# Routing tail of three expert layers: first pass's rows by a 0/1 product, slots inside its gate product, modulation rows loaded at two times

## The chip, the core and the metric

One program on one core of a Trainium2 chip. The time is the device time of the whole program in microseconds (us); lower is better. The profiler records one execution: every instruction of the engines PE (matrix products), DVE (vector), ACT (scalar), POOL (general) and SP (issues loads and stores), and every DMA packet.

## The reference, cut to what matters

A block with a mixer and a mixture of experts, then two more layers (attention and a mixture of experts each) whose inputs are scaled and shifted by rows made from a condition vector `c`. There are 512 tokens of 1024 numbers, 16 experts, and each token goes to two experts of one group.

```python
mod = c_act @ w_ada[i] + b_ada[i]
sh1, sc1, g1, sh2, sc2, g2 = [m[:, None, :] for m in jnp.split(mod, 6, axis=-1)]
...
group_p, group_idx = lax.top_k(jax.nn.softmax(group_logits, axis=-1), 1)
exp_p, exp_idx = lax.top_k(jax.nn.softmax(in_group, axis=-1), TOP_K_IN_GROUP)
combine = jnp.sum(jax.nn.one_hot(expert_id, N_EXPERTS) * gate[..., None], axis=1)
h = jax.nn.silu(jnp.einsum("td,edf->tef", t, expert_w_gate)) * jnp.einsum("td,edf->tef", t, expert_w_up)
y = jnp.einsum("tef,efd->td", h * combine[:, :, None], expert_w_down)
```

## The kernel before, in words

All is float32; one product of 128x128 by 512 columns is two PE instructions. The program is a row of blocks in which each engine has its own list of instructions, written out in order; engines wait for one another by semaphores. Within an engine nothing overtakes.

An expert layer is the function `moe` (L1303), called three times: in the first block (with `mod=0`), in the fox layer (`mod=1`) and in the last layer (no `mod`). The text calls them the first, second and third expert layer. It has two blocks.

The first block makes the normalised rows `x_tok`, stores them to `x_rows` in memory (SP, L1656), and routes: DVE finds each token's two experts (chain "route"), PE counts with triangular and all-one matrices which place a token has in its expert's list (the **ranks**, L1466 and L1468, in `bank[7]`). Then the tail of the routing: DVE turns ranks to 0/1 rows over 128 places (chain "pick", L1591), PE multiplies them with token numbers (L1475), and DVE has the token of each place of experts 0 and 1 (`slot_tok`, L1600). POOL gathers pass 0's and pass 1's rows by it from `x_rows` (`load_x`, L2081). Chains "order", "slots" and "expert" sort the other twelve experts by their counts and give each token a place in a **pass**.

A pass is 128 rows: one expert of up to 128 tokens or two of up to 64. There are 13, numbered 0 to 12 (`PASSES`). Passes 2 to 12 get their rows from four gathers of quarter rows each (L2076), whose addresses (`part_rows`) come from two small PE products, `pass_slots` (L1829) and `parts` (L1836). In the second block PE runs, for each pass `e`: the gate and up product (`gate_up`, L1708, eight steps of k), the down product of the pass before (`end`, L1721), the turn of this pass's hidden rows (`turn_h`, L1713). Ahead of pass 0 it makes `pass_slots`, the turn of pass 0's gathered rows (`turn_x`, L1693) and `parts`, with filler products (`keep_clock`, L1864) between them. DVE's list in that block is `slots_of_passes`, `rows_of_tokens`, `weights_of_tokens` (L2002 to L1994 in the order of the run), then for each pass the product of gate and up (`times_up`, L1732), the next pass's rows, the copies of the outputs (L1740, L1741) and of the turned rows (L1735). ACT applies silu (L1729) and issues the expert weights on its own DMA queue, each when its place of five is free: the gate and up weights after the gate product of the place's last user, the down weights after its down product. Outputs of a pass are stored by ACT (L1909) from one of two buffers, so the copies of pass 10 wait for pass 8's store to land.

In the first two layers SP also loads what the next layer's modulation needs (`modulation_loads`, L1291): 1536 of `b_ada` to each of four partitions, and six blocks of 128x1024 partial sums (`ada_part`), which it issues when the gate product of pass 10 is done and the last expert's gate and up weights have landed; in the first layer two norm rows (`ln2_loads`) follow, then the next stage's first weights. DVE adds the bias (`add_bias`, L2046, two steps each behind passes 11 and 12), waiting for all these loads:

```python
BIAS_AT = {NP - 2: (0, 1), NP - 1: (2, 3)}
...
slots_of_passes()
rows_of_tokens()
weights_of_tokens()
for e in range(NP):
    body(e)
```

## Time and profile before

| what | value |
|---|---|
| runs (3) | 2012.82, 2014.77, 2016.58 us; median 2014.77 |
| the profiled execution | 2019.38 us; its span 2017.6 us |
| PE busy | 1926.7 us, 95% of the span |
| DVE, ACT, POOL busy | 951.1, 435.5, 326.8 us |
| mean granted clock of PE | 0.979 of full |
| moved by DMA | 363.87 MB, 180 GB/s in the mean |

The span runs from the first to the last instruction; the execution's own time has 1.8 us more around it. A busy PE is one that has a product in flight, at whatever clock; the granted clock is given apart. The mean of the DMA hides that it is idle in the attention stages and full in the expert layers.

### The profile page before, as it was taken

What the parts mean: (1) busy time and instruction counts of PE and PEld (TensorE: products, weight loads), DVE (VectorE), ACT (ScalarE), POOL (GpSimd) and SP (SyncE); (2) the same over time, 40 slices, a digit from 0 to 9 for tenths busy, and PEclk for the clock granted to TensorE, in tenths of its full rate; (3) what the DMA queues carried; (4) which work ended last, traced back from release to release, by engine and by line L of the source; (5) the groups of instructions that cost most, each with busy time, mean ns of one, the idle gap of its engine ahead of it and who ended that gap; (6) DMA issues with size and microseconds to landing.
All of it is one profiled execution on the core that took longest, in us unless ns stands there. A gap on an engine that the chain in (4) does not pass through costs nothing. (4 is left out here: it accounts for less than half of the span.)

```text
span 2017.6 us, 20813 instructions
## 1 busy us (share of the span) xinstructions
PE 1926.7 (95%) x7482; PEld 1022.3 (51%) x7482; DVE 951.1 (47%) x1803; ACT 435.5 (22%) x1051; POOL 326.8 (16%) x548
## 2 busy tenths in 40 slices
PE   8999999999999999999799998999997999999995
PEld 4444444558885444543345445545433656645441
DVE  3443734547776022633363555535334367625333
ACT  1111101013333100110151105511001546612000
POOL 1000000000002000133010006502332003301333
PEclk9999999999999999999898999999997999999997
DMA  5222373730003125599844782137996202046996
GB/s 193 102 104 103 137 257 114 255 137 1 1 1 124 45 103 196 198 345 391 335 154 146 273 331 85 56 153 274 351 412 259 70 24 84 2 169 247 331 406 248
DMA packets 123401, 363.87 MB, mean 180 GB/s; under 512 B 26572, under 2 KB 31976, under 8 KB 110752
## 3 DMA queue, kind: packets, MB, share of 16 engines
q1 hardware_dynamic: 83200, 196.16, 27.0%
q10 hardware_dynamic: 26064, 133.70, 16.9%
q0 software_dynamic: 14032, 32.64, 4.6%
q8 instruction: 62, 1.02, 0.2%
q14 instruction: 43, 0.35, 0.1%
HBM read 335.07 MB, written 39.88 MB: 186 GB/s over the span
## 5 line engine op out<-in xcount | busy, mean ns | idle before, releaser
L447 PE MATMUL bank<-featT,ring 128*128 128x512 f32 x384 | 170.4, 597 | 3.0 <-DMA ring<-in_w_in 3.0
L2583 PE MATMUL bank<-ring,featT 128*128 128x512 f32 x384 | 168.9, 601 | 2.2 <-DVE small L2675 1.6
L1416 PE MATMUL bank<-ring,work 128*128 128x512 f32 x384 | 166.5, 593 | 3.0 <-PEq L1198 1.0
L1708 PE MATMUL bank<-work 128*128 128x512 f32 x384 | 168.8, 592 | 0.0
L2076 POOL DMA_INDIRECT work<-x_rows,small x132 | 131.7, 998 | 218.4 <-DVE work L2040 155.4
L2583 PEld LDWEIGHTS bank<-ring,featT 128*128 128x128 f32 x384 | 73.5, 193 | 93.4 <-issue 91.6
L1416 PEld LDWEIGHTS bank<-ring,work 128*128 128x128 f32 x384 | 72.2, 190 | 91.2 <-issue 91.2
L1732 DVE TENSOR_TENSOR work<-work,bank 128x256 f32<-128x256 f32 x39 | 16.5, 422 | 213.9 <-ACT work L1729 213.8
L447 PEld LDWEIGHTS bank<-featT,ring 128*128 128x128 f32 x384 | 71.8, 192 | 85.0 <-issue 81.9
L1708 PEld LDWEIGHTS bank<-work 128*128 128x128 f32 x384 | 71.1, 190 | 80.4 <-issue 80.4
L546 PE MATMUL bank<-ring,featT 128*128 128x512 f32 x256 | 110.4, 593 | 0.9 <-PEq L427 0.9
L1708 PE MATMUL bank<-ring,work 128*64 128x512 f32 (+1 forms) x384 | 106.2, 595 | 0.8 <-DVE work L1726 0.8
L1721 PE MATMUL bank<-work 128*128 128x512 f32 x184 | 88.6, 624 | 1.8 <-DVE work L1735 1.8
L1729 ACT ACTIVATE work<-bank 128x256 f32<-128x256 f32 x39 | 14.9, 383 | 323.4 <-PE bank L1708 323.4
L1100 PE MATMUL bank<-ring,featT 128*128 128x512 f32 x192 | 83.3, 593 | 1.0 <-PEq L830 1.0
L546 PEld LDWEIGHTS bank<-ring,featT 128*128 128x128 f32 x256 | 48.5, 190 | 61.4 <-issue 61.4
L301 DVE SCALAR_TENSOR_TENSOR ring_halves<-ring_halves,ismall 128x1024 f32<-128x1024 f32 x48 | 61.6, 1283 | 34.2 <-DMA ring_halves<-in_w_ada 30.7
L468 DVE TENSOR_SCALAR work<-bank,small 128x512 f32<-128x512 f32 x24 | 18.0, 751 | 107.6 <-PE bank L447 107.6
L1708 PEld LDWEIGHTS bank<-ring,work 128*64 128x64 f32 (+1 forms) x384 | 37.9, 150 | 60.5 <-issue 60.5
L2040 DVE STREAM_TRANSPOSE work<-work 128x1024 f32<-128x1024 f32 x33 | 66.9, 2028 | 0.0
L1721 PEld LDWEIGHTS bank<-work 128*128 128x128 f32 x184 | 35.6, 199 | 51.0 <-issue 51.0
L1100 PEld LDWEIGHTS bank<-ring,featT 128*128 128x128 f32 x192 | 36.1, 190 | 44.7 <-issue 44.7
(507 smaller groups left out, 3067.2 us busy)
## 6 DMA issues: line engine op xcount, KB each, us to landing
ring<-in_w_in SPq DMA_DIRECT2D x15, 2048.0 KB, 11.6
ring_halves<-in_w_ada SPq DMA_DIRECT2D x48, 512.0 KB, 6.5
y_rows<-work ACTq DMA_DIRECT2D x39, 512.0 KB, 11.6
state<-in_w_ada SPq DMA_DIRECT2D x24, 512.0 KB, 6.8
ada_w<-in_w_ada SPq DMA_DIRECT2D x24, 512.0 KB, 6.5
ring<-in_fox_w_in SPq DMA_DIRECT2D x6, 2048.0 KB, 11.7
work<-in_moe_w_gate ACTq DMA_DIRECT2D x12, 1024.0 KB, 7.2
work<-in_moe_w_up ACTq DMA_DIRECT2D x12, 1024.0 KB, 10.4
```

The lines of the kernel that those rows point to most:

```text
L301: DV.done(nc.vector.scalar_tensor_tensor(out=acc, in0=w, scalar=c_cols[:, k:k + 1], in1=acc, op0=ALU.mult, op1=ALU.add), ("slab", i))
L447: last = nc.tensor.matmul(bank[b % 4][:, :], w[:, k, (b % 4) * P:(b % 4 + 1) * P], featT[:, k, :], start=(k == 0), stop=(k == KD - 1))
L468: DV.done(nc.vector.tensor_scalar(acc, src[:, :], conv_cols[:, CONV - 1, b:b + 1], None, ALU.mult), ("tap0", b))
L546: last = nc.tensor.matmul(uv_bank(j)[:, :], featT[:, k, t * P:(t + 1) * P], w[:, k, :], start=(k == 0), stop=(k == KD - 1))
L1100: last = nc.tensor.matmul(zg_bank(j)[:, :], featT[:, k, t * P:(t + 1) * P], w[:, k, :], start=(k == 0), stop=(k == KD - 1))
L1416: last = nc.tensor.matmul(bank[j % 4][:, :], outT[:, k, t * P:(t + 1) * P], w[:, k, :], start=(k == 0), stop=(k == KD - 1))
L1708: last = nc.tensor.matmul(gu_sum[par][at], xgT[par][:, k, at], w_gu[place_of[u]][:, k, :, :], start=(k == 0), stop=(k == KD - 1))
L1721: last = nc.tensor.matmul(y_bank(e, h)[at, :], hT[par][:, k, at], w_dn[place_of[u]][k][:, span(h)], start=(k == 0), stop=(k == KF - 1))
L1732: return nc.vector.tensor_tensor(h_tok[par], act_g[par], bank[2 + par][:, FF:2 * FF], ALU.mult)
L2040: nc.vector.transpose(xgT[par].rearrange("p k (s b) -> p s k b", s=NQ), xg[par].rearrange("p (s a k) -> p s k a", s=NQ, k=KD)).then_inc(M_ ...
L2076: nc.gpsimd.indirect_dma_start(out=xg[par][:, s * QD:(s + 1) * QD], out_offset=None, in_=x_quarters, in_offset=bass.IndirectOffsetOnAxis(a ...
L2583: last = nc.tensor.matmul(f_bank(j)[:, :], featT[:, k, t * P:(t + 1) * P], w[:, k, :], start=(k == 0), stop=(k == KD - 1))
```

## The change

For each of the three expert layers:

- `x_rows` places of experts 0 and 1 are kept as one 0/1 matrix each, `is_listed` (places along the columns, tokens along the rows). Pass 0's rows are no longer gathered: PE multiplies the normalised rows by `is_listed[0]` (`first_rows`), 8 blocks by 4 token tiles, which gives them turned already. `slot_tok` holds pass 1's tokens alone (`second_list`).
- The chains "slots" and "expert" move to the second block, and the copy of pass 0's rows and `slot_tok` stand among them. `pass_slots` and `parts` move inside pass 0's gate product, ahead of its steps k = 4 and k = 6. Of the nine filler products behind the ranks, seven go.
- The partial sums 4 and 5 (after the norm rows in the first layer) are issued after the down product of pass 4; 0 to 3 when the gate product of pass 10 is done, with no wait for the last expert's weights. The bias steps are 1024 wide: one behind pass 9, one behind pass 10, three behind pass 11, one behind pass 12.

```diff
-        def modulation_loads(sp, l, places_free):
-            for i in range(4):
-                load(sp, b_ada[32 * i:32 * i + 1, :], D["b_ada_2"][l:l + 1, i * B_ADA:(i + 1) * B_ADA])
+        def modulation_loads(sp, l, after_fifth, places_free):
+            for i in range(6):
+                sp.dma_start(b_row(i), D["b_ada_2"][l:l + 1, i * DM:(i + 1) * DM]).then_inc(first_rows_landed, 16)
...
+            after_fifth()
+            for i in (4, 5):
+                sp.dma_start(ada_sum[:, i * DM:(i + 1) * DM], ada_part[l, :, i * DM:(i + 1) * DM]).then_inc(first_rows_landed, 16)
             places_free()
-            for i in range(6):
+            for i in range(4):
                 load(sp, ada_sum[:, i * DM:(i + 1) * DM], ada_part[l, :, i * DM:(i + 1) * DM])
...
-            BIAS_AT = {NP - 2: (0, 1), NP - 1: (2, 3)}
+            BIAS_AT = {NP - 4: (4,), NP - 3: (5,), NP - 2: (0, 1, 2), NP - 1: (3,)}
...
-                    keep_clock(2)
-                    for a in range(2 * T):
...
-                    keep_clock(4)
+                    keep_clock(1)
...
-                    link(V.tensor_tensor(two(prod2), two(O12), bcast(ranks.unsqueeze(1), P, 2, T * NE), ALU.mult))
-                    link(V.reduce_sum(rank_of, prod2.rearrange("p (a n) -> p a n", n=NE), X_AXIS))
...
+                    link(V.scalar_tensor_tensor(out=slot_at, in0=t16(ranks)[:, :, 0:N_WHOLE], scalar=1.0, in1=t16(O5[:, 0:T * NE])[:, :, 0:N_WHOLE], op0=ALU.add, op1=ALU.mult))
+                    for i in range(N_WHOLE):
+                        link(V.scalar_tensor_tensor(out=is_listed[i].rearrange("p (t n) -> p t n", t=T), in0=bcast(iota.unsqueeze(1), P, T, P), scalar=1.0,
+                                                    in1=bcast(slot_at[:, :, i:i + 1], P, T, P), op0=ALU.add, op1=ALU.is_equal))
...
+                    link(G.memset(xg[0], 0.0))
...
-                def gate_up(e, par):
+                def gate_up(e, par, between={}):
                     for k in range(KD):
+                        if k in between:
+                            between[k]()
...
+                    def first_rows():
+                        DV.wait(pe, ("pick", 1))
+                        for k in range(KD):
+                            for t in tiles:
+                                last = nc.tensor.matmul(bank[k // 4][:, (k % 4) * P:(k % 4 + 1) * P], eighth(x_tok[:, t, :], k), is_listed[0][:, t * P:(t + 1) * P],
+                                                        start=(t == 0), stop=(t == T - 1))
+                        last.then_inc(M_xT.sem, 1)
+
+                    def second_list():
+                        DV.wait(pe, ("pick", 2))
+                        for t in tiles:
+                            last = nc.tensor.matmul(bank[6][:, P:P + 1], is_listed[1][:, t * P:(t + 1) * P], tok_id[:, t:t + 1], start=(t == 0), stop=(t == T - 1))
+                        PE.done(last, "slots")
...
-                        gate_up(e, par)
+                        gate_up(e, par, {4: pass_slots, 6: parts} if e == 0 else {})
...
-                    keep_clock(1)
-                    pass_slots()
-                    keep_clock(1)
-                    turn_x(pe, 0, 0, 0)
-                    parts()
+                    first_rows()
+                    second_list()
                     keep_clock(1)
...
-                        def places_free():
-                            sp.wait_ge(M_gu.sem, v(M_gu, pass_of[users[3][-1]]))
-                            wait_gate_up(sp, NE - 1)
-                        modulation_loads(sp, mod, places_free)
-                    if late:
-                        late(sp)
+                        def after_fifth():
+                            sp.wait_ge(M_down.sem, v(M_down, pass_of[users[4][-1]]))
+                            if late:
+                                late(sp)
+                        modulation_loads(sp, mod, after_fifth, lambda: sp.wait_ge(M_gu.sem, v(M_gu, pass_of[users[3][-1]])))
...
+                    act.wait_ge(x_stored, 16 * T * (nth + 1))
                     keep_x_act(0)
...
+                    def slots_and_experts():
...
+                        dve.wait_ge(x_stored, 16 * T * (nth + 1))
+                        keep_x_dve(0)
+                        PE.wait(dve, "slots")
+                        DV.done(V.tensor_copy(slot_tok, bank[6][:, P:P + 1]), "slot_tok")
...
                         DV.done(V.tensor_copy(slot_f, bank[6][:, 2 * P:2 * P + NP]), "slot_f")
-                        keep_x_dve(0)
                         PE.wait(dve, "parts")
...
+                    slots_and_experts()
                     slots_of_passes()
                     rows_of_tokens()
                     weights_of_tokens()
...
-                    load_x(0, 0)
                     load_x(1, 1)
```

How the instructions move, at three places. On PE, first expert layer, from the start of the second block; L1864 is the filler product, L1829 `pass_slots`, L1693 the turn of gathered rows, L1836 `parts`, L1708 the gate product. Before:

```order
L1864 MATMUL bank<-level_mask,ident 128x512
L1829 MATMUL bank<-featT,work 128x13 [waits dve_steps]
L1829 MATMUL bank<-featT,work 128x13 x3
L1829 MATMUL bank<-featT,work 128x13 [waits dve_steps]
L1829 MATMUL bank<-featT,work 128x13 x3
L1864 MATMUL bank<-level_mask,ident 128x512
L1693 MATMUL bank<-ident,work 128x128 [waits moe_x_landed0]
L1693 MATMUL bank<-ident,work 128x128 x7
L1836 MATMUL bank<-featT 128x13 [waits act_steps,dve_steps]
L1836 MATMUL bank<-featT 128x13 x3
L1864 MATMUL bank<-level_mask,ident 128x512
L1708 MATMUL bank<-ring,work 128x512 [waits moe_x_kept_act,moe_x_kept_dve,slot0_landed]
```

Now, from the second step of the gate product (L1680) on; L1801 is `pass_slots`, L1808 `parts`, L1663 the turn of pass 1's rows, L1685 the turn of pass 0's hidden rows:

```order
L1680 MATMUL bank<-ring,work 128x512 x3
L1801 MATMUL bank<-featT,work 128x13 [waits dve_steps]
L1801 MATMUL bank<-featT,work 128x13 x3
L1801 MATMUL bank<-featT,work 128x13 [waits dve_steps]
L1801 MATMUL bank<-featT,work 128x13 x3
L1680 MATMUL bank<-ring,work 128x512 x2
L1808 MATMUL bank<-featT 128x13 [waits act_steps,dve_steps]
L1808 MATMUL bank<-featT 128x13 x3
L1680 MATMUL bank<-ring,work 128x512 x2
L1663 MATMUL bank<-ident,work 128x128 [waits moe_x_landed1]
L1663 MATMUL bank<-ident,work 128x128 x7
L1685 MATMUL bank<-ident,work 128x128 [waits moe_h]
```

Slots and parts have gone from ahead of the gate product to between its steps.

On DVE, first expert layer, the second block from its first chain's last step to the part rows; L1698 is the copy of pass 0's rows, L1971 `slot_tok`, L1975 the slots' 0/1 rows, L2013 the copy of the slots, L2015 and L2017 the part rows:

```order
L1967 SCALAR_TENSOR_TENSOR featT<-featT 128x8 [waits dve_steps]
L1698 COPY work<-bank 128x512 [waits moe_x_turned,moe_x_stored,dve_steps]
L1971 CAST ismall<-bank 128x1 [waits pe_steps]
L1972 TENSOR_TENSOR featT<-featT,small 128x104
L1973 TENSOR_TENSOR featT<-featT,small 128x104 [waits dve_steps]
L1975 TENSOR_TENSOR work<-work,featT 128x512 [waits dve_steps] x2
L1977 TENSOR_TENSOR featT<-featT,small 128x144 [waits dve_steps]
L1978 TENSOR_REDUCE featT<-featT 128x12 [waits dve_steps]
L1979 CAST ismall<-featT 128x12 [waits dve_steps]
L2013 COPY featT<-bank 128x13 [waits pe_steps,dve_steps]
L2015 TENSOR_SCALAR featT<-bank,small 128x52 [waits pe_steps]
L2017 CAST small<-featT 128x52 [waits dve_steps]
```

Before, the slots and experts stood at the end of the first block (L1622 is their last step), and the second began with the copy of the slots (L1999), pass 0's rows (L1726) and the part rows (L2002):

```order
L1621 TENSOR_REDUCE featT<-featT 128x12 [waits dve_steps]
L1622 CAST ismall<-featT 128x12 [waits dve_steps]
L1965 UNCONDITIONAL_BRANCH [waits dve_steps]
L1999 COPY featT<-bank 128x13 [waits pe_steps]
L1726 COPY work<-bank 128x512 [waits moe_x_turned]
L2002 TENSOR_SCALAR featT<-bank,small 128x52 [waits pe_steps]
L2004 CAST small<-featT 128x52 [waits dve_steps]
```

Slots and experts have come in ahead of the copy of the slots. What follows the part rows on DVE is the same in both: rows and weights of tokens, then `times_up` of pass 0.

On SP, first expert layer, from the norm row on (L202 is the helper `load`, L1302 the two early sums). Before:

```order
L202 DMA featT<-in_ffn_norm 128x1024
L202 DMA work<-ada_part 128x1024 [waits moe_gate_up_sum,far_gate_up_landed0,ada_stored1,ada_stored0]
L202 DMA work<-ada_part 128x1024 x5
L202 DMA work<-in_ln_g 128x1024
L202 DMA work<-in_ln_b 128x1024
L120 DMA ring<-in_fox_w_in 128x8x512 [waits moe_gate_up_sum]
```

Now:

```order
L202 DMA featT<-in_ffn_norm 128x1024
L202 DMA work<-in_ln_g 128x1024 [waits moe_down_sum,ada_stored1,ada_stored0]
L202 DMA work<-in_ln_b 128x1024
L1302 DMA work<-ada_part 128x1024 x2
L202 DMA work<-ada_part 128x1024 [waits moe_gate_up_sum]
L202 DMA work<-ada_part 128x1024 x3
L120 DMA ring<-in_fox_w_in 128x8x512 [waits moe_gate_up_sum]
```

Two norm rows and two sums have moved ahead, to the wait for a down product; the wait for landed weights is gone.

## Rows read from the trace of the kernel before

**Rows 1.** Windows; after each engine's busy us: PEclk, DMA share, GB/s.
```profile
912.00:977.00 65.00, 65.00 (x206) 25.89 (x205) 20.93 (x25) 5.88 (x12) 19.95 (x20) 1.00 1.01 406
1533.00:1540.30 7.30, 6.62 (x10) 2.60 (x10) 5.12 (x5) 0.00 (x0) 0.00 (x0) 0.60 0.18 72
```

**Rows 2.** Timeline, first expert layer's routing and pass 0: start, us, engine, line.
```profile
837.23 0.45 PE L1466 MATMUL bank<-work,strict 128*128 128x80 f32 x2 [0.32 <-DVE work L1579]
...
839.27 1.42 DVE L1591 TENSOR_TENSOR work<-work,small 128x512 f32<-128x512 f32 x2
...
851.16 0.27 DVE L2002 TENSOR_SCALAR featT<-bank,small 128x52 f32<-128x52 f32 x1
...
851.92 7.03 PE L1708 MATMUL bank<-ring,work 128*128 128x512 f32 x16
...
858.88 0.17 DVE L1994 CAST ismall<-small 128x8 int32<-128x8 f32 x1
...
859.95 0.44 PE L1713 MATMUL bank<-ident,work 128*128 128x128 f32 x2
```

**Rows 3.** Timeline of PE, 128x128 products back to back.
```profile
537.00 1.95 PE L868 MATMUL bank<-work 128*128 128x128 f32 x16
```

**Rows 4.** Timeline of PE, second expert layer: ranks, then pass 0's turn.
```profile
1373.81 0.45 PE L1466 MATMUL bank<-work,strict 128*128 128x80 f32 x2 [0.32 <-DVE work L1579]
...
1398.70 0.44 PE L1713 MATMUL bank<-ident,work 128*128 128x128 f32 x2
```

**Rows 5.** Timeline of PE, third expert layer: the same two places.
```profile
1837.33 0.45 PE L1466 MATMUL bank<-work,strict 128*128 128x80 f32 x2 [0.33 <-DVE work L1579]
...
1860.01 0.44 PE L1713 MATMUL bank<-ident,work 128*128 128x128 f32 x2
```

**Rows 6.** Timeline, first expert layer, passes 10 to 12.
```profile
963.79 0.38 ACT L1729 ACTIVATE work<-bank 128x256 f32<-128x256 f32 x1 [6.63 <-PE bank L1708]
...
970.53 3.19 SPq L202 DMA_DIRECT2D work<-ada_part  x6
...
978.11 7.03 PE L1708 MATMUL bank<-work 128*128 128x512 f32 x16
...
979.08 0.69 DVE L1741 COPY work<-bank 128x512 f32<-128x512 f32 x1 [1.84 <-DMA y_rows<-work]
...
993.63 3.52 DVE L2046 TENSOR_TENSOR work<-work,featT 1x1536 f32<-1x1536 f32 x2 [13.53 <-DMA work<-in_ln_b]
...
997.67 0.69 PE L1713 MATMUL bank<-ident,work 128*128 128x128 f32 x2 [8.95 <-DVE work L1732]
```

**Rows 7.** Timeline of PE, first expert layer, last down products, whole.
```profile
998.97 5.67 PE L1721 MATMUL bank<-work 128*128 128x512 f32 x8 [0.61 <-DVE work L1735]
```

**Rows 8.** Timeline, second expert layer, the same passes.
```profile
1508.53 2.82 SPq L202 DMA_DIRECT2D work<-ada_part  x6
...
1516.85 7.03 PE L1708 MATMUL bank<-work 128*128 128x512 f32 x16
1517.16 1.29 DVE L1740 TENSOR_TENSOR work<-bank,work 128x512 f32<-128x512 f32 x2 [1.18 <-DMA y_rows<-work]
...
1533.05 0.69 PE L1713 MATMUL bank<-ident,work 128*128 128x128 f32 x2 [5.58 <-DVE work L1732]
...
1534.34 5.93 PE L1721 MATMUL bank<-work 128*128 128x512 f32 x8 [0.61 <-DVE work L1735]
```

**Rows 9.** Timeline of PE, third expert layer, pass 12 (no modulation there).
```profile
1978.17 7.03 PE L1708 MATMUL bank<-work 128*128 128x512 f32 x16
...
1989.76 3.67 PE L1721 MATMUL bank<-work 128*128 128x512 f32 x8 [0.61 <-DVE work L1735]
```

**Rows 10.** DMA queues, 970.6 to 974: q1 is SP's, q10 ACT's, q0 POOL's.
```profile
q10 hardware_dynamic: 367, 1.39, 101.3%
```

**Rows 11.** DMA queues, 974 to 983: packets, MB, share of 16 engines.
```profile
q1 hardware_dynamic: 556, 2.06, 55.9%
q10 hardware_dynamic: 477, 1.72, 46.8%
```

More of the change, by code:

```diff
@@ L1470, in _ @@
                     PE.done(last, "ranks")
-                    keep_clock(2)
-                    for a in range(2 * T):
-                        if a in (0, T):
-                            DV.wait(pe, ("pick", N_PICK - 2 + a // T))
-                        last = nc.tensor.matmul(bank[6][:, P:P + N_WHOLE], slot_is[:, a * P:(a + 1) * P], tok_of[:, a * N_WHOLE:(a + 1) * N_WHOLE], start=(a == 0), stop=(a == 2 * T - 1))
-                    PE.done(last, "slots")
-                    keep_clock(4)
+                    keep_clock(1)
                 @block.scalar
```

86 lines of the change are left out of this document (44 added, 42 removed).

## The prediction

> **What bounds the kernel now.** I read the page's busy times first, then the windows, then the timeline of the three expert layers, PE and DVE side by side. PE is busy in 95% of the span, and inside the passes it is the bound: in the stretch 912 to 977 it is busy in every microsecond at the full clock, while the 16 DMA engines are full too, 406 GB/s at a share of 1.01 [rows 1]. So time can be won or lost in two sorts of places only: where PE waits, or where a load comes later than its use. The change touches two. One is the routing ahead of pass 0: from the ranks (L1466, 837.23) to the turned gate product of pass 0 (L1713, 859.95) 22.7 us go by in the first expert layer [rows 2], 22.7 in the third [rows 5], 24.9 in the second [rows 4]. The other is the end of the first two layers: there PE stands idle for 8.95 us [rows 6] and 5.58 us [rows 8] ahead of the last turn, because DVE has the bias rows in front of the last pass's product and the rows have not landed (the row at 993.63 waited 13.53 us for a load). The third layer, which has no modulation, shows the same passes without it [rows 9].
>
> **Routing, to the start of pass 0.** Removed are five DVE steps and a gather with its eight turns; added are one small step and two 512-wide comparisons. Two such comparisons took 1.42 us, from 839.27 on [rows 2] and behind two small steps; with one step ahead of them the first list is ready at about 839.5. Then PE makes pass 0's rows: 32 products of 128x128, two instructions each. Sixteen such instructions took 1.95 us of which about 0.28 is the last one's length, so 0.111 us each [rows 3]; 64 take 7.1 us, and the rows stand in the bank at 846.9. Copying them (0.7) hides beside the second list (8 x 0.111 = 0.9) and one filler product (about 0.95); the gate product starts at about 848.6 in place of 851.92 [rows 2]: 3.3 us earlier.
>
> **Routing, inside pass 0.** The 24 instructions for slots and parts, which stood ahead of the gate product, now stand inside it: 24 x 0.111 = 2.7 us. So it ends at 848.6 + 7.0 + 2.7 = 858.3, about 0.6 us earlier than before. The parts end at 856.6, after three quarters of the product (5.2) and the 2.7. What matters is who waits for them. On DVE everything from the part rows to the last cast of the weights of tokens stands, before and after, between the parts and the product of gate and up that PE's turn needs (the order on DVE). That stretch lasts from 851.16 to 859.05, 7.9 us [rows 2]; before, it lay beside the whole gate product and ended with it. Now it starts 5.5 us later, because the parts come at the sixth of eight steps. It ends at 864.5, the product of gate and up 0.5 later, and PE turns at 865.05 in place of 859.95: **+5.1 us**. ACT has no say: its two exponentials and its table load lie inside the same stretch. Every later pass moves with it, since PE is full there. The third layer has the same pace, +5.1. In the second the stretch took 2.2 us longer before; I take the new one at the pace of the others, since 64 wide products replace the light ones there: +2.9. Sum **+13.1**.
>
> **The clock after that wait.** PE has its gate product and the turn of pass 1 done at 859.2 and then nothing for 5.8 us. No stretch before has such a gap in the middle of a layer; the nearest is the 5.58 us at the second layer's end [rows 8]. After it the mean granted clock was 0.60 of full speed, so mostly the lower level, 1.2 GHz [rows 1], and the turn took 0.69 and the eight down instructions 5.93, against 0.44 [rows 2] and 3.67 [rows 9]: 2.5 us. Bounds: 0 if the clock holds; 3.5 if a whole gate product (7.03) runs at half. I take 2.5, the row with the nearest gap: three times, **+7.5** (0 to 10.5).
>
> **The modulation rows.** Before, six rows (and in the first layer two norm rows) were issued when the last expert's weights had landed, 970.53 and 1508.53 [rows 6, 8]. From the last gate product's start to the last down product's end the first layer needs 998.97 + 5.67 - 978.11 = 26.5 us [rows 6, 7], the second 23.4 [rows 8], the third 15.3 [rows 9]. All that could be won is 11.2 and 8.1. But the bytes stay the same. Four loads of 0.52 MB (first layer; two in the second) now go out after the fifth pass, where the engines are full; at 406 GB/s they take 5.2 us (2.6), by which all later loads of ACT's queue come later. The other four go out when pass 10's gate product ends, 963.8, and no longer wait for the last expert's weights. SP's traffic appeared 3.5 us after its issue [rows 6, 10], and then the two queues shared the engines about evenly, 55.9% and 46.8% [rows 11].
> First layer: at 967.3 the last expert's weights had 3.2 us to go; with the 5.2 that makes 8.4, at half speed beside 5.2 of SP's, then beside the next stage's weights. They land between 980.9 (if those keep out) and 984, and PE wants them at 978.1 [rows 6]: about 5 late. The output of pass 8, whose landing (979.08) frees the buffer for pass 10's, lands at 979.1 - 2.5 (what SP had taken before) + 3 x 5.2 = 992.2, so the down products of pass 11 start at about 992.9 in place of 985.1: 7.8 late in all. The five idle microseconds lower the clock, 2. New: 15.3 + 7.8 + 2 = 25.1, **-1.4**.
> Second layer: the weights land as they are wanted, pass 8's output at 1517.2 - 2.6 + 2.6 + 5.2 + 2.9 = 1525.3, with its copy 2.8 late; 1 for the clock. New 19.1, **-4.3**. Bounds for both: nothing won, or all 19.3.
> The Trainium skill (DMA: Bandwidth & Descriptors, Where 436 GB/s comes from) holds that between HBM and SBUF the HBM's share of about 358 GB/s binds. The trace shows more, 406 GB/s over 65 us [rows 1], and the measurement decides; with 358 each 5.2 would be 5.9, an estimate, and the sum some 3 us higher.
>
> **At no cost, with their cover.** The memset of the row buffer and the missing gather lie on POOL, idle at that time. Pass 1's gather starts later but has the longer pass 0 ahead of its turn; were that gone, its flight would show. The quarter gathers of passes 2 on start 5 us later, for a use a pass later; the fifth expert's weights 1 us later, for a use four passes later. The wait for the stored rows ended long before the copies. The four early bias steps lie where DVE idles in each pass.
>
> **Sum.** 13.1 + 7.5 - 1.4 - 4.3 = +14.9. The profiled execution took 2019.38, its span 2017.6; it would take 2034. The median of the three runs lies 4.6 below it, so I forecast 2014.77 + 14.9 = **2029.7 us**. A measurement of this kernel can tell about 0.2%, 4 us, from no change.
>
> **The rivals.**
> *The rows are hidden in full.* The weights of experts 13 to 15 and pass 8's output land in time in spite of the earlier loads; it decides at 978.1 and 985.1 in the first layer. For it: no PE wait on a load inside a layer, and 7.6 us between landing and use for the last weights [rows 6]. Against it: the full engines [rows 1, 11]. Then the ends give 19.3: 13.1 + 7.5 - 19.3 = +1.3, 2016, no change; if the clock holds as well, -6.2, 2008.6, faster.
> *The clock holds through the routing wait.* Place: the 5.8 us behind pass 0's gate product. Against it stands the 5.58 us gap. +7.4, 2022.
> *Loads late in more passes.* The 5.2 us of backlog also delays experts 9 to 14, each wait with its clock; price the upper bounds, 13.1 + 10.5 and nothing won, about +24, 2039.
> *The slots hide as named.* The move inside the gate product would cost only its 2.7 us if DVE's tail came behind pass 0's product of gate and up. The order excludes it, so it has no chance of its own.
>
> **How the numbers follow.** My forecast 0.54 (its own range 2022 to 2037), the rows hidden 0.27, of which 0.14 faster, 0.12 the same and 0.01 slower, the clock holding 0.10, more loads late 0.09. Faster 0.14, same 0.12, slower 0.74. The range 2008.5 to 2041 takes in all four cases and leaves out a tenth or so at the two ends.
>
> **What would show it.** Right: in each layer a PE wait of 5 to 6 us ahead of pass 0's turn, ended by DVE, and slow products behind it; no bias step that waits for a load; in the first layer a wait for weights at pass 12. Wrong: pass 0's turn at most 23 us after the ranks (then the DVE stretch is not what PE waits for), or the last pass as short as in the third layer, 15.3 (then the loads do not collide).

## The result, and the profile after

The changed kernel takes 2049.07 us (median of 4 runs, 2048.18 to 2053.36), the kernel before 2014.67 (4 runs): **1.75% slower**, ratio 1.0175 with an interval of 1.0157 to 1.0192. The forecast was 2029.7 with a range up to 2041. The side was right, the size was not: +34.4 us where +14.9 stood. One execution of those behind all the numbers here, of the run s_fill6 below, took 4102.86 us, twice the others, for a reason not known, and stands in no median and no ratio. The profiled execution took 2049.17 us with a span of 2047.4; against the profiled execution of before, whose own time lay 4.6 above its median, the span grew by 29.8. Cut at places that both kernels have, it grew here (us):

| stretch | before | after | difference |
|---|---|---|---|
| start to the ranks of the first layer | 837.2 | 836.1 | -1.1 |
| ranks to the turn of pass 0, first layer | 22.72 | 35.85 | +13.1 |
| that turn to the last gate product | 118.2 | 122.8 | +4.6 |
| last gate product to the end of the last down product | 26.5 | 22.1 | -4.5 |
| on to the ranks of the second layer | 369.2 | 365.5 | -3.6 |
| ranks to turn, second layer | 24.89 | 35.85 | +11.0 |
| turn to last gate product | 118.2 | 120.8 | +2.6 |
| last gate product to the end | 23.4 | 17.3 | -6.1 |
| on to the ranks of the third layer | 297.1 | 296.1 | -1.0 |
| ranks to turn, third layer | 22.68 | 35.83 | +13.2 |
| turn to the end of the span | 157.6 | 159.2 | +1.6 |

The -3.6 lies in the fox layer, which the change does not touch: from its first projection to the next ranks the profiles of these kernels take between 344.5 and 348.5, and the one of before, 348.2, is near the upper end. The rest is the routing, three times, and the ends of two layers.

First the routing, PE's timeline in the first layer, which answers to [rows 2] (start, us, engine, line, tiles and shapes, count; in brackets the idle time ahead and what ended it):

```profile
836.13 0.45 PE L1471 MATMUL bank<-work,strict 128*128 128x80 f32 x2 [0.32 <-DVE work L1577]
...
838.48 15.50 PE L1815 MATMUL bank<-work,resid 128*128 128x128 f32 x64
...
855.57 3.60 PE L1680 MATMUL bank<-ring,work 128*128 128x512 f32 x8
...
865.12 1.04 PE L1663 MATMUL bank<-ident,work 128*128 128x128 f32 x8
871.98 0.69 PE L1685 MATMUL bank<-ident,work 128*128 128x128 f32 x2 [5.82 <-DVE work L1704]
872.63 9.86 PE L1680 MATMUL bank<-ring,work 128*128 128x512 f32 x16
```

L1815 is `first_rows`: its 64 instructions take 15.50 us where the forecast had 7.1, and the gate product starts 19.4 us behind the ranks, 8.1 later than the forecast had it (848.6 less 837.23, 11.4). Behind that, all is as forecast: a wait of 5.82 ahead of the turn, ended by DVE, and a slow gate product of pass 1. The second and third layer show the same 15.50 and 5.8. A product has two operands: the stationary block, whose load is an instruction of its own (PEld), and the moving operand, whose columns the product's instruction counts. The loads, by shape, from 800 to 1000 us (busy us, mean ns):

```profile
L1680 PEld LDWEIGHTS bank<-work 128*128 128x128 f32 x125 | 23.1, 190 | 28.1 <-issue 26.1 <-DMA work<-in_expert_w_up 2.0
L1815 PEld LDWEIGHTS bank<-work,resid 128*128 128x128 f32 x64 | 15.3, 335 | 0.9 <-DVE work L1584 0.9
```

A block of the same shape is loaded in 190 ns by the gate products and in 335 ns here, one behind the other without a pause. DVE's timeline of the same stretch:

```profile
843.56 0.17 DVE L1967 SCALAR_TENSOR_TENSOR featT<-featT 128x8 f32<-128x8 f32 x1
854.12 0.69 DVE L1698 COPY work<-bank 128x512 f32<-128x512 f32 x1 [10.39 <-PE bank L1815]
...
863.51 0.27 DVE L2015 TENSOR_SCALAR featT<-bank,small 128x52 f32<-128x52 f32 x1 [2.37 <-PE bank L1808]
...
871.30 0.17 DVE L2008 CAST ismall<-small 128x8 int32<-128x8 f32 x1
871.50 0.42 DVE L1704 TENSOR_TENSOR work<-work,bank 128x256 f32<-128x256 f32 x1
```

DVE waits 10.39 us for these rows, with the last slots steps behind the copy; from the part rows (863.51) to the last cast of the weights (871.47) it takes 8.0 us, against the 7.9 of [rows 2]. Windows of the rows, of the wait and of what follows it. The last three numbers are the granted clock, the DMA share and the rate in GB/s:

```profile
838.40:846.00 7.60, 7.52 (x32) 7.52 (x32) 4.53 (x18) 0.00 (x0) 0.00 (x0) 1.00 0.01 2
846.00:854.00 8.00, 8.00 (x37) 8.00 (x36) 0.00 (x0) 0.00 (x0) 0.00 (x0) 1.00 0.00 0
866.00:872.00 6.00, 0.18 (x3) 0.02 (x1) 5.21 (x25) 2.58 (x5) 4.63 (x5) 0.95 0.77 277
872.00:878.00 6.00, 6.00 (x9) 2.57 (x10) 0.95 (x2) 0.00 (x0) 2.41 (x3) 0.50 0.86 312
```

The clock was full, 1.00, while the rows were made, so their double time is no fall of the clock, and the DMA was idle beside them. Behind the wait the clock is at the lower level, 1.2 GHz, for six microseconds. Pass 1's gate product takes 9.86, 9.81 and 8.61 in the three layers, and 7.03 at the full clock.

Last the ends of the first two layers, PE's timeline, against [rows 6 to 8]:

```profile
994.78 7.13 PE L1680 MATMUL bank<-work 128*128 128x512 f32 x16 [1.79 <-DMA work<-in_expert_w_up]
1005.85 6.34 PE L1693 MATMUL bank<-ring_halves,work 128*64 128x512 f32 x16 [3.94 <-DVE work L1707]
...
1013.17 3.67 PE L1693 MATMUL bank<-work 128*128 128x512 f32 x8 [0.61 <-DVE work L1707]
...
1539.01 7.03 PE L1680 MATMUL bank<-work 128*128 128x512 f32 x16
1547.70 3.65 PE L1693 MATMUL bank<-ring_halves,work 128*64 128x512 f32 x16 [1.66 <-DVE work L1707]
...
1552.65 3.67 PE L1693 MATMUL bank<-work 128*128 128x512 f32 x8 [0.61 <-DVE work L1707]
```

The 8.95 and 5.58 us ahead of the last turn are gone. New are a wait of 1.79 for the last expert's weights and waits of 3.94 and 1.66 ahead of the down products of pass 11; behind the longer one these products take 6.34 in place of 3.65.

### The profile page after: what moved, and what is told of

The parts are those of the page before. It is cut to its first block and busy times, and to the rows that moved or that the text cites. A ratio compares the mean times of both kernels' runs of the same rounds, so it can differ in the third digit from the quotient of the medians.

```text
span 2047.4 us, 21023 instructions
## 1 busy us (share of the span) xinstructions
PE 1948.2 (95%) x7584; PEld 1052.2 (51%) x7584; DVE 949.4 (46%) x1801; ACT 435.5 (21%) x1051; POOL 330.5 (16%) x548
## 5 line engine op out<-in xcount | busy, mean ns | idle before, releaser
L1680 PE MATMUL bank<-work 128*128 128x512 f32 x384 | 168.9, 593 | 1.8 <-DMA work<-in_expert_w_up 1.8
L1680 PE MATMUL bank<-ring,work 128*64 128x512 f32 (+1 forms) x384 | 114.6, 616 | 0.0
L1680 PEld LDWEIGHTS bank<-work 128*128 128x128 f32 x384 | 71.1, 190 | 82.4 <-issue 80.4
L1693 PE MATMUL bank<-work 128*128 128x512 f32 x184 | 84.4, 598 | 1.8 <-DVE work L1707 1.8
L1680 PEld LDWEIGHTS bank<-ring,work 128*64 128x64 f32 (+1 forms) x384 | 40.2, 158 | 61.3 <-issue 61.3
L1693 PE MATMUL bank<-ring_halves,work 128*64 128x512 f32 (+1 forms) x192 | 57.1, 627 | 5.6 <-DVE work L1707 5.6
## 6 DMA issues: line engine op xcount, KB each, us to landing
ring<-in_fox_w_in SPq DMA_DIRECT2D x6, 2048.0 KB, 11.4
work<-in_moe_w_up ACTq DMA_DIRECT2D x12, 1024.0 KB, 10.9
```

The source lines that it names most:

```text
L1680: last = nc.tensor.matmul(gu_sum[par][at], xgT[par][:, k, at], w_gu[place_of[u]][:, k, :, :], start=(k == 0), stop=(k == KD - 1))
L1693: last = nc.tensor.matmul(y_bank(e, h)[at, :], hT[par][:, k, at], w_dn[place_of[u]][k][:, span(h)], start=(k == 0), stop=(k == KF - 1))
```

## The experiments

Times are medians; a ratio is to runs of the kernel before on the same chip, whose median was 2016.6 to 2017.7 in these groups. The groups ran on different chips, so two runs of different groups are compared by their ratios; 0.001 of a ratio is 2 us.

### Why the rows took 15.5 us

One run (e_probe) measures the product by itself. Behind the ranks of the kernel before, runs of 32 products each, `every(x, k, s)` being 128 numbers of a row in steps of s:

```diff
+ for k in range(KD):
+     for t in tiles:
+         nc.tensor.matmul(bank[0][:, (k % 4) * P:(k % 4 + 1) * P], every(x_tok[:, t, :], k, 8), ident[:, :], start=(t == 0), stop=(t == T - 1))
```

and so with the other steps, with `start=True, stop=True` for single products, and once with the two operands exchanged.

> The kernel before, with seven extra runs of 32 products of 128x128 (64 instructions each) behind the ranks; their sums are thrown away, nothing else is changed. Stationary blocks: first layer, every 8th number of the normalised rows, once adding four products to a sum and once each product alone; second layer, neighbouring numbers, every 2nd number, and a run with the 0/1 unit matrix as stationary block and every 8th number as the moving operand; third layer, every 4th number adding up, and neighbouring numbers each alone. Theory S (the step of the stationary block sets the time): 15.5 us for both runs with step 8, 7.1 for neighbouring numbers and for the moving operand, steps 2 and 4 in between or at 7.1. Rival A (adding four products to one sum sets it): 15.5 for every run that adds up, whatever the step, 7.1 for the two runs of single products. Rival F (a new stationary block for every product sets it): 15.5 for all but the run with the unit matrix.

Measured, PE's timeline (L1483 step 8 adding up, L1486 step 8 each alone, L1490 neighbouring numbers, L1493 step 2, L1496 moving operand with step 8, L1500 step 4, L1503 neighbouring numbers each alone):

```profile
838.92 15.47 PE L1483 MATMUL bank<-ident,resid 128*128 128x128 f32 x64
854.24 15.40 PE L1486 MATMUL bank<-ident,resid 128*128 128x128 f32 x64
...
1406.20 7.39 PE L1490 MATMUL bank<-ident,work 128*128 128x128 f32 x64
1413.43 7.70 PE L1493 MATMUL bank<-ident,work 128*128 128x128 f32 x64
1420.97 15.09 PE L1496 MATMUL bank<-work,ident 128*128 128x128 f32 x64
...
1900.02 15.18 PE L1500 MATMUL bank<-ident,work 128*128 128x128 f32 x64
1915.03 7.31 PE L1503 MATMUL bank<-ident,work 128*128 128x128 f32 x64
```

The step decides; adding up and new blocks do not (rivals A and F fall: step 8 takes as long without adding up, and a new block for every product costs nothing with neighbouring numbers). Neighbouring numbers and step 2 take 7.3 to 7.7, steps 4 and 8 twice that. Theory S was wrong in two points. Step 4 pays in full, where 15.5 stood for step 8 alone. And the moving operand pays as much, 15.09; there the loads of the unit matrix stay at 209 ns, so it is not the load of the stationary block as such but the reading of either operand.

In the changed kernel itself, the same instructions on neighbouring numbers (run contig):

```diff
-  gu = [(lambda s, i=i: s[:, :].rearrange("p (g k n) -> p g k n", g=2, k=KD)[:, i, :, :], rows8(w[u]))
+  gu = [(lambda s, i=i: s[:, :].rearrange("p (g k n) -> p g k n", g=2, k=KD)[:, i, :, :], rows(w[u]) if u == 0 else rows8(w[u]))
...
-  last = nc.tensor.matmul(bank[k // 4][:, (k % 4) * P:(k % 4 + 1) * P], eighth(x_tok[:, t, :], k), is_listed[0][:, t * P:(t + 1) * P],
+  last = nc.tensor.matmul(bank[k // 4][:, (k % 4) * P:(k % 4 + 1) * P], x_tok[:, t, k * P:(k + 1) * P], is_listed[0][:, t * P:(t + 1) * P],
```

> The changed kernel with the stationary blocks of pass 0's rows made of 128 neighbouring numbers in place of every 8th, and expert 0's gate and up weights loaded in the row order that fits this; as many instructions of the same shapes. Theory: the step of 8 is all that made these 64 instructions take 15.5 us. They take 7.4, pass 0's turn comes 28 us behind the ranks in place of 35.8, and the kernel takes 2049 - 3 x 8 = about 2025, a little under the forecast. Rival: the loads of expert 0 in 1 KB rows come late or the products are slow for another reason, and it stays above 2040.

Measured: 2025.62 us, ratio 1.0044 (1.0029 to 1.0058). PE's timeline, first layer, whose ranks stood at 834.78:

```profile
837.12 7.41 PE L1815 MATMUL bank<-work,resid 128*128 128x128 f32 x64
...
862.53 0.69 PE L1685 MATMUL bank<-ident,work 128*128 128x128 f32 x2 [5.80 <-DVE work L1704]
863.17 9.39 PE L1680 MATMUL bank<-ring,work 128*128 128x512 f32 x16
```

27.75 us from ranks to turn, where the forecast had 27.8 (837.23 to 865.05). With this one price put right, the turn, the wait and the slow product come out as forecast. The whole time does not quite: +8.9 against this group's runs of before (2016.73), where the forecast had +14.9; the modulation part gave more than the forecast allowed it (below).

The other way round, with the rows as moving operand, 512 neighbouring numbers at a time (run swap):

```diff
-  for k in range(KD):
-      for t in tiles:
-          last = nc.tensor.matmul(bank[k // 4][:, (k % 4) * P:(k % 4 + 1) * P], eighth(x_tok[:, t, :], k), is_listed[0][:, t * P:(t + 1) * P],
-                                  start=(t == 0), stop=(t == T - 1))
+  for h in range(2):
+      for t in tiles:
+          last = nc.tensor.matmul(bank[h][:, :], is_listed[0][:, t * P:(t + 1) * P], x_tok[:, t, span(h)], start=(t == 0), stop=(t == T - 1))
```

ACT and DVE copy a half each to `xg[0]`, and eight turns follow, as for gathered rows.

> The changed kernel with pass 0's rows made the other way round: the 0/1 matrix is the stationary block and the normalised rows stream by, 512 at a time (16 instructions, by the gate product's rows 7.0 us), the rows come out unturned, are copied (0.7), turned (1.0) and copied again. The gate product then starts about 12 us after the list, where it starts 17 us after it in the changed kernel. Theory S: DVE's tail and its wait stay as they are, so pass 0's turn comes 6 to 7 us earlier than in the changed kernel, in all three layers: 2049 - 20 = about 2029, close to the forecast. If something else than these products made the changed kernel late (DVE's slots, the first rows' copies), the turn moves less than 3 us a layer: above 2040.

Measured: 2028.62 us, ratio 1.0051 (1.0034 to 1.0068), as expected of this run. That it lies so near 2029.7 is chance: its turn comes 28.9 us behind the ranks, 1.1 later than the forecast's, and its modulation part gives more. Its first layer, ranks at 837.90:

```profile
840.25 7.13 PE L1814 MATMUL bank<-resid,work 128*128 128x512 f32 x16
...
850.35 3.67 PE L1679 MATMUL bank<-ring,work 128*128 128x512 f32 x8
...
866.82 0.69 PE L1684 MATMUL bank<-ident,work 128*128 128x128 f32 x2 [5.80 <-DVE work L1703]
867.47 9.09 PE L1679 MATMUL bank<-ring,work 128*128 128x512 f32 x16
```

### The wait ahead of pass 0's turn, and the clock behind it

These runs start from swap. First the wait (run s_tail): the weights of tokens go behind pass 0.

```diff
-  weights_of_tokens()
-  for e in range(NP): body(e)
+  body(0)
+  weights_of_tokens()
+  for e in range(1, NP): body(e)
```

ACT's two exponentials go behind its own `body(0)` in the same way.

> The kernel called swap with the weights of tokens (4.3 us of DVE and ACT's two exponentials) moved behind pass 0's product of gate and up. Theory: that product waits for DVE's list and for nothing else, so pass 0's turn comes 4.2 us earlier in each layer (wait 5.8 down to 1.6), and with so short a wait the clock holds: swap - 12.6 - 5.5 = about 2010. Rival: something behind it on DVE or ACT (the exponentials' table loads, pass 1's silu) takes the place, and less than half of it is won: above 2020.

Measured: 2011.64 us, ratio 0.9971 (0.9958 to 0.9983), by the ratios 16 us below swap. The turn in the first layer, whose ranks stood at 835.15:

```profile
859.77 0.44 PE L1684 MATMUL bank<-ident,work 128*128 128x128 f32 x2 [1.51 <-DVE work L1703]
860.42 7.11 PE L1679 MATMUL bank<-ring,work 128*128 128x512 f32 x16 [0.21 <-issue]
...
1847.93 8.80 PE L1679 MATMUL bank<-ring,work 128*128 128x512 f32 x16 [0.21 <-issue]
```

24.6 in place of 28.9, in all three layers 24.6 or 24.7. DVE's list was what PE waited for. Behind the shorter wait the product is at full speed in the first two layers (7.11 in both); in the third (the last row) it takes 8.80 behind a wait of 1.56, so that the clock holds after a short wait is not shown. Then the clock (run s_fill): filler products in the wait.

```diff
+  if e == 0:
+      keep_clock(12)
   pe.wait_ge(M_h.sem, v(M_h, e))
   turn_h(e, par)
```

> The kernel called swap with 12 filler products of 128x512 (about 5.6 us) between the turn of pass 1's rows and the turn of pass 0's product, where PE waited 5.8 us. Theory: the wait stays as long, but the granted clock stays at the full level behind it; turn 0.44 in place of 0.69 and pass 1's gate product 7.1 in place of 8.4 to 9.1, about 1.9 a layer: swap less 5 to 6, about 2023. Rival: the slow product behind the wait comes from something else (late weights, memory traffic) and stays slow: no change.

Measured: 2033.12 us, ratio 1.0076 (1.0062 to 1.0091), not below swap as expected but by the ratios some 5 us above it. The gate product behind the fillers did take 7.03, but the fillers took 10.5 us: I had counted each as one instruction, and it is two. With six (run s_fill6):

> As s_fill, with 6 filler products in place of 12: one such product is two instructions of 0.43 us, so that 12 took 10.5 us and outlasted the wait of 5.8 by 4.7 a layer. Six take 5.2 and end before DVE does. Theory (the clock falls in the wait and costs 1.5 to 2.1 us in pass 1's gate product and 0.3 in the turn, each layer): swap less 6, about 2023, pass 1's gate product at 7.03. Rival: the products behind the wait are slow for the traffic beside them: no change against swap, 2028.6.

Measured: 2022.33 us (nine runs), ratio 1.0026 (1.0016 to 1.0036).

```profile
860.73 5.32 PE L1857 MATMUL bank<-level_mask,ident 128*128 128x512 f32 x12
866.69 0.44 PE L1684 MATMUL bank<-ident,work 128*128 128x128 f32 x2 [0.65 <-DVE work L1703]
867.34 7.11 PE L1679 MATMUL bank<-ring,work 128*128 128x512 f32 x16 [0.21 <-issue]
```

The turn comes no earlier (ranks at 837.77, so 28.9 as in swap), and the clock holds in all three layers. By the ratios the kernel is 5 us faster than swap, though their intervals just touch; by the profiles the three turns and gate products, 9.09, 8.36 and 8.66 in swap and 7.11 here, give 5.5. That is the price of the three falls of the clock there.

### The modulation part alone

The kernel before with the modulation hunks of the change (the diff above, from `modulation_loads` to `add_bias`), and the changed kernel with those of before (runs mod_only and router_only).

> The kernel before with the change's modulation loads and bias steps alone, its routing left as it was. Theory: the ends of the first two layers gain what they gain in the changed kernel (last gate product to last down product 22.1 in place of 26.5, 17.3 in place of 23.4) and a load wait of some 2 us is given back: about -8 to -10, 2005 to 2007, with the idle time ahead of the last turn gone. Rival (the forecast's own term): late weights and the late output of pass 8 take most of it, -5.7, 2009. Rival: with the routing of before all loads of the last passes come later than their use, and nothing is won: 2015.

> The changed kernel with the modulation loads and bias steps of before: the routing part of the change alone. Theory: it costs the whole of the loss and what the modulation wins comes on top: ranks to pass 0's turn 35.8 us in every layer, a slower gate product of pass 1 behind it, ends of the first two layers as before (26.5 and 23.4): 2014.7 + 37 + 7 = about 2058. Rival: the modulation part is neutral or harmful in the changed kernel, and this one takes 2049 or less.

Measured: the modulation alone 2005.82 us, ratio 0.9953 (0.9937 to 0.9968), so 6 to 13 us faster; the routing alone 2061.61, ratio 1.0229 (1.0212 to 1.0246). The two parts pull in opposite ways, and the small one had hidden behind the large one. They add up: against this group's 2016.67, +44.9 and -10.9 make +34, and the whole change measured +34.4. PE in the first layer's end, modulation alone:

```profile
977.41 3.67 PE L1725 MATMUL bank<-work 128*128 128x512 f32 x8 [1.18 <-DVE work L1739]
...
983.35 7.13 PE L1712 MATMUL bank<-work 128*128 128x512 f32 x16 [2.04 <-DMA work<-in_expert_w_up]
994.41 5.35 PE L1725 MATMUL bank<-ring_halves,work 128*64 128x512 f32 x16 [3.93 <-DVE work L1739]
```

and what DVE itself waited for, ahead of the copy that freed the last of them:

```profile
993.18 0.69 DVE L1745 COPY work<-bank 128x512 f32<-128x512 f32 x1 [12.23 <-DMA y_rows<-work]
```

It is the landing of pass 8's output, as the forecast named it: issued at 963.33, landed at 993.2. The 1.18 is the same thing one pass earlier, pass 7's output, which the forecast had not named.

If the lateness comes from loads that go out too early, putting back the wait for the last expert's weights must end it. Sums 4 and 5 and the norm rows are left early (run mod_wait):

```diff
   def places_free():
       sp.wait_ge(M_gu.sem, v(M_gu, pass_of[users[3][-1]]))
+      wait_gate_up(sp, NE - 1)
```

> The kernel mod_only with the wait of before put back: the four late sums are issued when the last expert's weights have landed, not at pass 10's gate product; the norm rows and two sums stay early. Theory: in mod_only these four loads share the engines with the last expert's weights (PE waits 2.0 for them at pass 12) and with the stored output of pass 8 (PE waits 1.2 and 3.9 for its buffer). With the wait, weights and output land in time, and the sums still land before pass 12's product: last gate product to last down product 16 to 18 us in the first layer in place of 21, 16 in the second in place of 17; mod_only less 5 to 8, about 1999. Rival: the sums then land too late and DVE's bias steps hold up pass 12's product as in the kernel before: 2006 or more.

Measured: 2003.53 us, ratio 0.9939 (0.9925 to 0.9952), about 3 less than the modulation alone by the ratios, whose intervals overlap, where 5 to 8 were expected. Weights and output land in time (in the first layer no wait for the weights is left, and 0.41 in place of 3.93 ahead of pass 11's down products), so the early loads were the cause, but (DVE's timeline, then PE's)

```profile
986.53 3.71 DVE L2056 TENSOR_TENSOR work<-work,featT 1x1024 f32<-1x1024 f32 x3 [4.45 <-DMA work<-ada_part]
```
```profile
990.74 0.69 PE L1717 MATMUL bank<-ident,work 128*128 128x128 f32 x2 [4.80 <-DVE work L1736]
```

the three bias steps now wait for the sums in front of pass 12's product, the fault of the kernel before in small. They are moved behind pass 12 (run mod_last):

```diff
-  BIAS_AT = {NP - 4: (4,), NP - 3: (5,), NP - 2: (0, 1, 2), NP - 1: (3,)}
+  BIAS_AT = {NP - 4: (4,), NP - 3: (5,), NP - 1: (0, 1, 2, 3)}
```

> The kernel mod_wait with its four late bias steps all behind the last pass's turned product (in mod_wait three of them stood in front of pass 12's product of gate and up, waited 4.45 us for the sums in the first layer, 3.9 in the second, and took 3.7 more; PE waited 4.8 and 1.9 and its last down products ran at the lower clock, 5.9 and 5.4 in place of 3.7). Theory: pass 12 then runs as in the third layer, last gate product to last down product 15.5 to 16 us in both layers in place of 23.0 and 18.9, and the four steps lie beside the last down products, with 1 to 2 us given back to the last copies: mod_wait less 6 to 9, about 1996. Rival: the steps then hold up the last copies of the outputs and the sums of the next stage by as much as they held up pass 12: 2002 or more.

Measured: 2001.48 us, ratio **0.9926** (0.9912 to 0.9939), faster than both kernels. Of the 6 to 9 expected about 2 came, and they are not clear of mod_wait's interval: pass 12 runs as in the third layer (15.9 and 15.3 from its gate product to the last down product's end), but the four steps hold up the last copy of the outputs, and the next stage's sums wait for it, 6.13 where it was 2.55 (in the second layer 5.67 for 3.43):

```profile
989.83 3.67 PE L1725 MATMUL bank<-work 128*128 128x512 f32 x8 [0.61 <-DVE work L1739]
999.64 7.05 PE L2197 MATMUL bank<-work,ones 128*128 128x512 f32 x12 [6.13 <-PEq L1398]
```
```profile
992.14 4.95 DVE L2056 TENSOR_TENSOR work<-work,featT 1x1024 f32<-1x1024 f32 x4
997.13 0.69 DVE L1745 COPY work<-bank 128x512 f32<-128x512 f32 x1
```

### Can the routing part be made to pay?

From swap and s_tail (run best1): the 0/1 matrices in a buffer of their own, so that DVE makes all slots while PE makes the rows, and slots and parts ahead of the gate product again.

```diff
-  gate_up(e, par, {4: pass_slots, 6: parts} if e == 0 else {})
+  gate_up(e, par)
...
   first_rows()
   second_list()
+  pass_slots()
+  turn_first()
+  parts()
   keep_clock(1)
```

> The changed kernel with four things altered: pass 0's rows with the 0/1 matrix as stationary block (as in swap); this matrix in a buffer of its own, so that all of DVE's slots come while PE makes the rows; slots and parts ahead of the gate product again, in the time of the rows' copies; the weights of tokens behind pass 0's product (as in s_tail). Theory: the gate product starts at about 11.5 us behind the ranks (14.7 in the kernel before, 19.4 in the changed one) and pass 0's turn comes at about 19.5 (22.7 before), with no slow clock: against the run with the modulation part alone (2005.8) 3 x 3 less, about 1997. Rival: DVE's rows of tokens and part rows still end after the gate product, and it lands at 2005.

Measured: 2009.98 us (2003.34 to 2018.18 over 12 runs), ratio 0.9965 (0.9951 to 0.9979), where 1997 was expected; by the ratios it is 2 us above the modulation part alone (0.9953), and the intervals overlap. The windows of the first layer show a loss (the clock is the third number from the end):

```profile
847.40:850.00 2.60, 2.60 (x26) 2.60 (x24) 1.90 (x6) 0.60 (x1) 0.58 (x1) 1.00 0.03 6
...
851.00:852.00 1.00, 1.00 (x9) 1.00 (x8) 0.69 (x1) 0.60 (x1) 0.00 (x0) 0.62 0.64 213
852.00:854.10 2.10, 2.10 (x5) 1.07 (x6) 1.43 (x8) 0.00 (x0) 0.36 (x1) 0.50 0.76 207
```

PE has no idle moment there; it makes products of 1, 13 and 128 columns, and the clock falls to half. In the first two layers pass 0's turn comes 26 us behind the ranks. In the third, with the same products, the clock held in this execution, and the turn comes at 22.65, which is what the kernel before needs and not the 19.5 of the expectation: the gate product starts 14.6 us behind the ranks even there and not 11.5, since the list, the slots, the turn, the parts and a filler fill 5.3 us ahead of it. The fillers of before, put back between the narrow products (run best1_fill):

```diff
+  keep_clock(1)
   pass_slots()
+  keep_clock(1)
   turn_first()
```

> The kernel best1 with two filler products put between its narrow products (one ahead of the slots, one behind them), as the kernel before has them. In best1 the granted clock fell to the lower level about 3.5 us into a row of 48 instructions of 1 to 128 columns, although PE had no idle moment, and pass 0's gate product took 8.1 to 9.0. Theory: the narrow products let the clock fall, and the fillers keep it: the gate product takes 7.03, it costs 0.9 to 1.8 for the fillers and wins 1.5 ahead of the gate product and 1 to 2 in it: best1 less 3 to 6, about 2005. Rival: the fall comes from elsewhere, and the fillers only add their time: 2014.

Measured: 2011.11 us (2008.29 to 2011.60), ratio 0.9966 (0.9953 to 0.9979). The clock stays at 1.00 and the gate product at 7.03 in all three layers of the profiled execution, with 24.4 from ranks to turn; best1's three had a mean of 24.9, so the gain that was expected did not come. That the narrow products bring the fall and the fillers prevent it is not shown. Best1's third layer had these products and no fall, and the kernel before had these fillers in its second layer and a fall (its windows, then PE's timeline, the filler behind the slots, 2.06 where 1.10 is usual):

```profile
1386.00:1387.00 1.00, 1.00 (x2) 0.26 (x2) 0.00 (x0) 0.00 (x0) 0.00 (x0) 0.50 0.00 0
```
```profile
1385.55 2.06 PE L1864 MATMUL bank<-level_mask,ident 128*128 128x512 f32 x2
```

No version with the rows by products was faster than the gather with the same modulation part (0.9953); for s_tail, best1 and best1_fill the intervals overlap with it, so that they are as fast is not excluded.

## Why the prediction was wrong in its size

**The step that failed** is "64 take 7.1 us, and the rows stand in the bank at 846.9". The durations were those of [rows 3], products of the same shape whose stationary block lies in neighbouring numbers. The new ones read every eighth. They took 15.5, 8.4 more, and the turn of pass 0 came 8.0 us later than forecast in each layer (35.85 behind the ranks, forecast 27.8), 24 in all. The forecast took the nearest row for the price and gave it no bounds, though no product of the trace of before (the turns aside) reads an operand with that step; all its ranges were put on later steps. The turns could not have warned of it: those of gathered rows read with that step, and eight of them take 1.05 (L1693 at 849.27 before), no longer than others. Its signs of being right all came (a wait of 5.8 ended by DVE, slow products behind it, a wait for weights at pass 12), since none of them looked at the rows. With twice that row as the upper bound, 7.1 more in each layer, the range would have ended at 2041 + 21 = 2062 and held the result, though the product itself took 2.2 times the row.

The step's cost has a rule in the Trainium skill (SBUF — State Buffer, Door 1: The DMA port swizzle, the note on "cachelines"): a line of SBUF has 16 bytes, and a reader needs at least two hits in a line for full speed. The probe agrees: two numbers per 16 bytes 7.70, one 15.18. The same note counts a step of four float32 as free; here it is the first of the four steps measured that doubles the time, and the measurement decides.

**DVE's tail, right.** "It ends at 864.5 ... PE turns at 865.05": with the price of the rows put right, the turn came at 27.75 us behind the ranks (contig), 27.8 in the forecast; the wait was 5.80, forecast 5.8; moving the tail away (s_tail) took the wait away. The credit for the second layer, +2.9 in place of +5.1, holds for the one profiled execution and not for the kernel: its 24.9 held a fall of the clock (0.50 from 1386 to 1387, 0.72 on to 1390), and the three later profiles with the routing of before (mod_only, mod_wait, mod_last) have 22.67 or 22.68 there.

**The clock, right.** Forecast 2.5 a layer. From pass 0's turn to pass 1's the three layers take 2.7, 2.6 and 1.4 more than before, 6.8 in all against 7.5. The fillers (s_fill6) show it by itself, 5.5 us on swap, whose product was less slow (9.1, 8.4, 8.7). The bound of 3.5 was mis-worked: a gate product of 7.03 run wholly at half the clock would lose 7. It was not passed because the clock was back at 0.98 from 878 on, inside the product.

**The modulation, right in its mechanism, too small.** Forecast -5.7; alone it gave 6 to 13 by the runs, 8.1 by the profiles from pass 0's turn to the layers' ends (1.8 and 6.3). The named lateness was there: forecast 7.8 late in all in the first layer, and 2.04 + 1.18 + 3.93 = 7.2 measured (mod_only), of which the weights were 2.0 and not 5; the slower down product behind it lost 1.7 (5.35 for 3.65), forecast 2. In the second layer 1.4 and 0.25 in place of 2.8, with no loss of clock.

**The sum by measured terms.** 37.2 for the three routings, 6.8 for the clock, 1.8 for the weights and -10.6 for the two ends make +35.2, where the forecast had 13.1 + 7.5 - 5.7 = 14.9. Of the 20.3 between them the rows are 24, and the clock and the modulation part take off 0.7 and 3.1. The fox layer and the stretches ahead of the ranks take 5.7 off between these two profiles, so that the span grew by 29.8. By the medians it is +34.4.

**The rivals.** The rows hidden in full did not come: 1.79 and 3.94 us of waits for a load and a store are left in the first layer. The clock did not hold. More loads late did not come either: the stretch from pass 0's turn to the last gate product grew by 4.6 in the first layer, 2.7 of it up to pass 1's turn and 1.8 the last weights. None of the three decides the size; the rival that was missing is a product slower than its shape.

## What to carry to other kernels

Take a product's price only from a row whose operands lie in memory in the same way; where none does, give it a bound well above the row (here it took 2.2 times the row), and find the smaller layout change (here the other operand order, or the weights' row order) before giving the product up. A cheap gather that runs beside other work need not be replaced: made on PE, even at full speed, the same rows brought pass 0's turn no earlier (22.65 us behind the ranks in best1's third layer, 22.7 before). A load that is moved ahead of its competitors should still wait for those that are needed first (mod_wait). The steps that use it belong behind the last work that others wait for; here mod_last put them ahead of the last copy of the outputs, and the next stage waited 3.6 us longer. A place behind that copy was not tried.

## What the runs showed of the hardware

- Products of 128x128 by 128 columns, 64 instructions: 7.39 us with neighbouring numbers, 7.70 with step 2, 15.18 with step 4, 15.47 with step 8; step 8 on the moving side 15.09 (e_probe, the granted clock at 1.00 in each). The turns of gathered rows, which also read every eighth number, are not slower (L1663 in the changed kernel, eight in 1.04) than turns of neighbouring ones (L2212 of the kernel before, eight in 1.07 and 1.09); why is left open.
- The granted clock fell to the lower level while PE was busy without a gap, behind a few microseconds of products of 1 to 128 columns, in two of three layers of one execution of best1 and not in the third. With two 512-wide fillers between them it stayed at 1.00 in all three layers of one execution of best1_fill; in the kernel before, which has such fillers, it fell in one layer of three (there PE had stood idle for 0.63 us, some 2 us earlier).
- One filler of 128x512 in float32 is two instructions, 0.87 to 0.89 us (s_fill 10.47 us for 12, s_fill6 5.32 for six).
